# VectorE's order moved at the output projection, at the seam of two layers and at the router of a two-layer decoder trunk

## The chip, the core and the metric

One Trainium2 chip, one core. The time is the device time of one launch in microseconds (us). Engine names of the profile: PE is TensorE (PEld its weight loads), DVE VectorE, ACT ScalarE, POOL GpSimd, SP SyncE. A name with q (DVEq, ACTq) is the engine's instruction queue, where semaphore increments and waits run.

## The reference

512 tokens of width 1024 pass two residual layers, all in fp32:

```python
for layer in range(2):
    h = rms_norm(x, attn_norm[layer])
    x = x + (hgrn2_diff_mixer(h, ...) if layer % 2 == 0 else gla_mixer(h, ...))
    h = rms_norm(x, ffn_norm[layer])
    x = x + hierarchical_moe(h, ...)
```

Both mixers end with `merge_heads(rms_norm(o)) * silu(g)`, times an output weight of 1024x1024. The mixture of experts picks one of 4 groups and then 2 of its 4 experts for each token, with a weight from two softmaxes. Each of the 16 experts is `(silu(h @ w_gate) * (h @ w_up)) @ w_down` with 1024x512, 1024x512 and 512x1024 weights.

## The kernel before, in words

**Three products for one.** A large fp32 product is made of three faster fp32r products: each operand is split into a high part, which ScalarE rounds off by a copy to fp32r, and a low part, which VectorE makes as operand minus high part. `three` (lines 1091 to 1096) issues the products; one step of it covers 128 rows of the contraction. A wait for a "low half" is thus a wait for VectorE.

**Order by lists.** What each engine does in a layer up to the router is written as a list of steps (`mixer_steps`, `norm_steps`). Every engine walks the same list in order and does its own part of each step, so moving a step moves it on all of them, SP and GpSimd included. `with_splits` puts the four pieces ("split") of the next 1024x512 weight group ahead of the last two of the four product units (one unit is 128 rows of output) of a group. Queues are in order, and engines wait for each other by semaphores.

**Output projection.** For each of four token tiles i: step `out` makes the head outputs (TensorE) and, on ScalarE, VectorE and GpSimd, their norm: ScalarE squares into the single buffer `exp_tmp`, VectorE sums, GpSimd takes the power -0.5 (line 765), VectorE multiplies into G (line 1465). Step `oT` transposes G (TensorE, line 1120), copies the high half (ScalarE, line 902) and makes the low half (VectorE, line 1559). Its transposes use PSUM banks 2 and 3 in each tile, so tile i+1 needs the low half of tile i done. Step `wo` is the product (24 steps of TensorE) and the add to x (VectorE, line 1722). `gw` multiplies the gates by the norm weight (line 1604). `out` of tiles 0 and 2 and of 1 and 3 share PSUM banks. The first expert's gate weight is loaded by SP when `out` of tile 3 is done.

**Seam** (from layer 0's experts to layer 1's first product, `norm_steps(2)`). `x` i adds the two gathered expert rows of tile i to x (line 1510, two instructions), `p` i adds the last expert's rows (line 1519), which TensorE makes as a product with a one-hot matrix (line 1435, four instructions for a tile). `stat` i squares x (ScalarE), `h` i is the norm (lines 1454, 765, 1542), `hT` i its transpose and two halves. Before the change TensorE makes the products of all four `p` in a row ahead of the list, with banks 0-1, 4-5, 2-3 and again 4-5.

**Router and first expert.** VectorE, in order: one-hot matrices, `first_low(1, ...)` (low halves of the first expert's up weight, line 1529), `idx` to GpSimd, which gathers the first expert's rows by DMA; then token weights and the last expert's one-hot (lines 1783 to 1795, `last_ready`); then the *lists*: slots of each token and the list of further blocks (lines 1797 to 1829, `eid_ready`), 32 instructions; then `rows_T(0, 0)` and `rows_T(1, 1)`, the low halves of the gathered rows of experts 0 and 1 (line 1844); `low(GATE)`, four low halves of expert 1's gate weight (line 1836); `times_up(0)`, silu(gate) times up (line 1857, `act_ready`); then the expert loop, whose `block_ve` begins with `low(DOWN)`, four low halves of the down weight, and the low half of the activations (line 1869). TensorE, in order: rows 0 transposed, gate product of expert 0, rows 1 transposed, one-hot transposed (needs `last_ready`), up product 0; then in `block_pe(0)`: gate product of expert 1, in whose middle, after 12 of 24 steps, stand the transposes of expert 0's activations (`act_T`, needs `act_ready`), rows 2 transposed, down product 0, up product 1, and so on. `slot` and `eid` are read at the end of the experts only.

Of the kernel before, what the change touches and what calls it, by code (L numbers as in the profile page):

```python
# [87 lines left out]
def build(nc, t):  # L88
# [37 lines left out]
    def mixer_steps(l):  # L126
# [9 lines left out]
        if l == 0:  # L136
# [26 lines left out]
            steps += [dS[0], dS[1], out[0], fill.pop(0), dS[2], out[1], fill.pop(0)] + weighted[2:4]  # L163
        else:
# [19 lines left out]
        out, oT, wo = ([(*k, i) for i in range(NT)] for k in (("out", l), ("oT", l), ("wo", l, 0)))  # L184
        steps += [out[2], oT[0], out[3], oT[1], wo[0], oT[2], wo[1], oT[3], wo[2], wo[3]]
# [7 lines left out]
    def norm_steps(n):  # L193
# [4 lines left out]
        if n == 0:  # L198
# [3 lines left out]
        return [x[0], x[1], own[0], p[0], p[1], own[1], stat[0], h[0], own[2], own[3], x[2], hT[0], stat[1], halves[0],  # L202
                h[1], p[2], x[3], hT[1], stat[2], u[0], p[3], h[2], hT[2], stat[3], u[1], h[3], hT[3], u[2],
# [31 lines left out]
    with ctx:  # L235
# [207 lines left out]
        for l in range(NL):  # L443
# [59 lines left out]
            for i in range(NT):  # L503
                bk.plan(("P", l, i), ([0, 1], [4, 5], [2, 3], [4, 5])[i])
# [218 lines left out]
        def _(pool):  # L723
# [52 lines left out]
            for l in range(NL):  # L776
                for s in STEPS[l]:
# [6 lines left out]
                    elif s[0] == "out" or s[0] == "da" and s[2] >= 3 and (s[2] - 3) % NH == NH - 1:  # L784
# [28 lines left out]
        def _(sc):  # L813
# [41 lines left out]
            for l in range(NL):  # L855
# [7 lines left out]
                for s in STEPS[l]:  # L863
# [95 lines left out]
                    elif kind == "out":  # L959
                        head_norm(s, DVS[l])  # L960
# [126 lines left out]
        def _(pe):  # L1087
# [9 lines left out]

            for l in range(NL):
# [3 lines left out]
                for s in STEPS[l]:  # L1102
                    kind = s[0]
                    if kind in ("hT", "oT", "xT"):
# [10 lines left out]
                        for g in range(2):  # L1115
# [5 lines left out]
                            ins.then_inc(bk.filled(k), 1)  # L1121
                    elif kind == "alpha":
# [305 lines left out]
                pe.wait_ge(bk.freed(("lastT", l)), bk.uses[("lastT", l)][1])  # L1428
                for i in range(NT):
                    key = ("P", l, i)  # L1430
                    bk.acquire(pe, key)
                    for c in range(2):
                        if i == 0:
                            pe.wait_ge(y_ready, 2 * l + c + 1)
                        ins = pe.matmul(PS[:, bk.uses[key][0] + c], lastT[:, i * P:(i + 1) * P],
                                        y_last[0:CAP, c * GC:(c + 1) * GC], start=True, stop=True)
                    ins.then_inc(bk.filled(key), 1)
# [3 lines left out]
        def _(ve):  # L1441
# [81 lines left out]
            for l in range(NL):  # L1523
# [7 lines left out]
                for s in STEPS[l]:  # L1531
# [152 lines left out]
                    elif kind == "out":  # L1684
                        i = s[2]
                        dv = DVS[l]
                        head_norm(wide(s, dv), dv, lambda c: G[:, i, c * dv:(c + 1) * dv], G[:, i, 0:NH * dv])
# [95 lines left out]
                ve.wait_ge(r_eg, l + 1)  # L1783
                link(red(r["gsum"], r["eg"], AX, ALU.add))
                ve.wait_ge(r_e2, l + 1)
                link(ts(r["den"], r["e2"], 1.0, None, ALU.add))
                link(tt(r["den"], r["den"], r["gsum"], ALU.mult))
                link(ve.reciprocal(r["wt"][:, 0], r["den"]))
                link(tt(r["wt"][:, 1], r["wt"][:, 0], r["e2"], ALU.mult))
                link(tt(r["w_of"], r["OH"][:, :, :, NE - 1], r["wt"], ALU.mult))  # L1790
                link(tt(r["w_last"], r["w_of"][:, 0], r["w_of"][:, 1], ALU.add))
                for i in range(NT):
                    ins = ts(ohj[:, i], iota_f[:, 0:CAP], rank[:, i, NE - 1:NE], r["M"][:, i, NE - 1:NE], ALU.is_equal, ALU.mult)
                link(ins)
                ve.sem_inc(last_ready, 1)

                link(ts(r["nx"], total, float(CAP), None, ALU.is_gt))
                for m in range(2, FULLS + 1):
                    link(stt(r["nx"], total, float(m * CAP), r["nx"], ALU.is_gt, ALU.add))
                link(ve.tensor_tensor_scan(r["off"], ones[:, 0:NE], r["nx"], 0.0, ALU.mult, ALU.add))  # L1800
                link(tt(r["off"], r["off"], r["nx"], ALU.subtract))
                link(ts(r["q"], rank, float(CAP), None, ALU.is_ge))

                link(tt(r["ein"][:, 0], r["off"], iota_f[:, 0:NE], ALU.subtract))
                link(ts(r["ein"][:, 0], r["ein"][:, 0], float(NE - 1), None, ALU.add))
                link(tt(r["b"], r["q"], r["ein"][:, 0:1].broadcast_to([P, NT, NE]), ALU.mult))
                for m in range(2, FULLS + 1):
                    link(stt(r["q"], rank, float(m * CAP), r["q"], ALU.is_ge, ALU.add))
                link(tt(r["b"], r["b"], r["q"], ALU.add))
                link(tt(r["b"], r["b"], iota_f[:, 0:NE].unsqueeze(1).broadcast_to([P, NT, NE]), ALU.add))  # L1810
                link(stt(r["j"], r["q"], -float(CAP), rank, ALU.mult, ALU.add))
                for of, by in (("bc", "b"), ("jc", "j")):
                    link(tt(r["tA"], r["OH"], r[by].unsqueeze(1).broadcast_to(both), ALU.mult))
                    link(red(r[of], r["tA"], AX, ALU.add))
                link(stt(r["jz"], r["bc"], float(NE - 1), r["jc"], ALU.not_equal, ALU.mult))
                link(stt(r["sl"], r["bc"], float(CAP), r["jz"], ALU.mult, ALU.add))
                link(cp(slot[:], r["sl"]))

                it8 = iota_f[:, 0:16].unsqueeze(2).broadcast_to([P, 16, NE])
                off8 = r["off"].unsqueeze(1).broadcast_to([P, 16, NE])  # L1820
                nx8 = r["nx"].unsqueeze(1).broadcast_to([P, 16, NE])
                link(tt(r["ein"], it8, off8, ALU.subtract))
                link(tt(r["ein2"], r["ein"], nx8, ALU.is_lt))
                link(stt(r["ein2"], r["ein"], 0.0, r["ein2"], ALU.is_ge, ALU.mult))
                link(tt(r["ein2"], r["ein2"], iota_f[:, 0:NE].unsqueeze(1).broadcast_to([P, 16, NE]), ALU.mult))
                link(red(r["eidf"], r["ein2"], AX, ALU.add))
                link(red(r["eidf"][:, 15:16], r["nx"], AX, ALU.add))
                link(cp(eid[:], r["eidf"]))
                ve.sem_inc(eid_ready, 1)

# [54 lines left out]
                rows_T(0, 0)  # L1885
# [42 lines left out]
```

## Time and profile before

| | us |
|---|---|
| median of 3 runs | 1304.54 (1303.98 to 1304.84) |
| profiled execution, device time | 1303.31 |
| its span | 1301.5 |
| PE, PEld busy | 1171.5, 886.2 |
| DVE, ACT, POOL busy | 916.6, 682.2, 95.5 |

The profile is of one execution. Its span runs from the first to the last instruction; the device time holds 1.8 us more. The stages follow each other in time: mixer of layer 0 up to 288 us, its output projection and router product up to 346, lists and first expert up to 391, experts up to 670, seam up to 709, and then the same for layer 1 (output projection 902, lists 965, experts 1003 to 1284). A row of a timeline gives start, duration, engine, line, operation, output and inputs, shape, how many instructions are merged, and in brackets how long the engine had been idle before it and who ended that.

### The profile page before, as it was taken

To read this page: it belongs to the slowest core of one execution; us is meant where nothing else is said; L and a number is where in the kernel's file an instruction comes from. 1 tells how busy PE (TensorE), PEld (TensorE's weight loads), DVE (VectorE), ACT (ScalarE), POOL (GpSimd) and SP (SyncE) were. 2 spreads that over 40 slices of the span, in tenths; PEclk is the share of its full clock that TensorE was granted. 3 is DMA by queue.
4 is the path that set the end of the run, shared out by engine and by line. 5 is a ranking of instruction groups with operands and counts; after the bars stand their busy time and mean duration, and the time that the engine had idled before them with its cause. 6 is when DMAs were issued, how large, how long until landed. Compare 5 with 4: busy or idle time off the path is not lost.

```text
span 1301.5 us, 16716 instructions
## 1 busy us (share of the span) xinstructions
PE 1171.5 (90%) x5676; PEld 886.2 (68%) x5676; DVE 916.6 (70%) x1247; ACT 682.2 (52%) x853; POOL 95.5 (7%) x132
## 2 busy tenths in 40 slices
PE   5998889979759999999987999998966999999995
PEld 4776578868636767666646678887854766676663
DVE  4656658564568888888976247646566888888886
ACT  4336751133327878777743251122323877878771
POOL 1120000010010000000030000001000000000003
PEclk9999999989869999999997999999977999999998
DMA  6231110131479999999960131113167999999955
GB/s 218 90 87 65 65 65 1 65 129 66 162 271 344 392 392 394 386 396 395 338 214 1 69 98 52 65 66 130 65 231 256 354 393 395 393 388 392 391 203 206
DMA packets 129644, 282.51 MB, mean 217 GB/s; under 512 B 18976, under 2 KB 19488, under 8 KB 129584
## 3 DMA queue, kind: packets, MB, share of 16 engines
q1 hardware_dynamic: 119680, 246.98, 51.4%
q0 software_dynamic: 6112, 21.76, 5.1%
q10 hardware_dynamic: 3792, 12.98, 2.6%
q8 instruction: 36, 0.59, 0.2%
q14 instruction: 24, 0.20, 0.0%
HBM read 262.83 MB, written 18.87 MB: 216 GB/s over the span
## 4 chain that ended last, share of the span: by engine, by line
PE 60%; DVE 22%; issue 10%; ACT 5%; POOL 1%; DVEq 1%; DMA 0%; ACTq 0%
PE PS L1094 18%; PE PS L1096 17%; PE PS L1095 17%; DVE expert_w_low L1836 6%; PE PS L1183 3%; PE PS L1120 2%; DVE group_low L1575 1%; ACT weight_high L861 1%; DVE G L1465 1%; DVE xgT_low L1844 1%; POOL rstd L765 1%; PE PS L1293 1%; DVE sum_sq L1461 1%; DVE act L1857 1%; DVE x_sb L1519 1%
## 5 line engine op out<-in xcount | busy, mean ns | idle before, releaser
L1836 DVE TENSOR_TENSOR expert_w_low<-expert_w,weight_high 128x1024 fp32r<-128x1024 f32 x368 | 426.3, 1220 | 73.2 <-ACT weight_high L861 70.8
L861 ACT ACTIVATE weight_high<-expert_w 128x1024 fp32r<-128x1024 f32 x384 | 374.9, 1048 | 64.6 <-PE PS L1096 56.3
L1094 PE MATMUL PS<-weight_high,xgT_high 128*96 128x512 f32 x512 | 205.7, 402 | 12.7 <-DVEq L1846 9.3
L1096 PE MATMUL PS<-weight_high,xgT_low 128*96 128x512 f32 x512 | 202.8, 396 | 0.0
L1095 PE MATMUL PS<-expert_w_low,xgT_high 128*96 128x512 f32 x512 | 202.4, 395 | 0.0
L1094 PE MATMUL PS<-group_high,hT_high 128*128 128x512 f32 x416 | 173.1, 416 | 11.6 <-DVEq L1562 4.5
L1095 PE MATMUL PS<-group_low,hT_high 128*128 128x512 f32 x416 | 166.7, 401 | 0.0
L1096 PE MATMUL PS<-group_high,hT_low 128*128 128x512 f32 x416 | 166.7, 401 | 0.0
L1094 PEld LDWEIGHTS PS<-weight_high,xgT_high 128*96 128x96 f32 x512 | 83.3, 163 | 47.4 <-DVEq L1846 9.9
L1094 PE MATMUL PS<-weight_high,actT_high 128*96 128x512 f32 x256 | 103.8, 405 | 9.1 <-DVEq L1871 8.5
L1575 DVE TENSOR_TENSOR group_low<-group_w,group_high 128x1024 fp32r<-128x1024 f32 x68 | 80.7, 1222 | 43.9 <-ACT group_high L885 41.2
L1096 PEld LDWEIGHTS PS<-weight_high,xgT_low 128*96 128x96 f32 x512 | 83.3, 163 | 36.6
L1095 PEld LDWEIGHTS PS<-expert_w_low,xgT_high 128*96 128x96 f32 x512 | 83.7, 164 | 33.6
L1096 PE MATMUL PS<-weight_high,actT_low 128*96 128x512 f32 x256 | 101.3, 396 | 0.0
L1095 PE MATMUL PS<-expert_w_low,actT_high 128*96 128x512 f32 x256 | 101.0, 394 | 0.0
L1094 PEld LDWEIGHTS PS<-group_high,hT_high 128*128 128x128 f32 x416 | 80.5, 193 | 29.5 <-issue 5.2
L1096 PEld LDWEIGHTS PS<-group_high,hT_low 128*128 128x128 f32 x416 | 79.9, 192 | 18.9
L1095 PEld LDWEIGHTS PS<-group_low,hT_high 128*128 128x128 f32 x416 | 80.5, 193 | 16.3
L885 ACT ACTIVATE group_high<-group_w 128x1024 fp32r<-128x1024 f32 x68 | 69.1, 1054 | 27.9 <-PE PS L1096 23.8
L1183 PEld LDWEIGHTS PS<-Q,K 128*128 128x128 f32 x512 | 61.0, 192 | 11.4 <-DVE K L1653 4.3
L1183 PE MATMUL PS<-Q,K 128*128 128x64 f32 (+1 forms) x512 | 61.4, 273 | 6.4 <-DVEq L1629 2.9
L1094 PEld LDWEIGHTS PS<-weight_high,actT_high 128*96 128x96 f32 x256 | 41.5, 162 | 30.4 <-DVEq L1871 5.9
(244 smaller groups left out, 1457.9 us busy)
## 6 DMA issues: line engine op xcount, KB each, us to landing
expert_w<-in_moe_w_gate SPq DMA_DIRECT2D x32, 2048.0 KB, 11.5
expert_w<-in_moe_w_up SPq DMA_DIRECT2D x32, 2048.0 KB, 10.4
expert_w<-in_moe_w_down SPq DMA_DIRECT2D x32, 2048.0 KB, 10.9
group_w<-in_even_w_in SPq DMA_DIRECT2D x6, 2048.0 KB, 7.8
group_w<-in_odd_w_in SPq DMA_DIRECT2D x6, 2048.0 KB, 7.9
y_rows<-yb ACTq DMA_DIRECT2D x30, 384.0 KB, 5.7
group_w<-in_even_w_out SPq DMA_DIRECT2D x2, 2048.0 KB, 7.7
h_rows<-h SPq DMA_DIRECT2D x8, 512.0 KB, 10.8
```

The source lines that it names most:

```text
L765: pool.tensor_tensor(dst, dst, neghalf[:, 0:dst.shape[-1]], ALU.pow).then_inc(root_ready, 1)
L861: act_(hi, w, ACT.Copy).then_inc(w_hi, 1)
L885: act_(hi, w, ACT.Copy).then_inc(g_hi_ready, 1)
L1094: pe.matmul(out, ah, bh, start=first, stop=False)
L1095: pe.matmul(out, ah, bl, start=False, stop=False)
L1096: return pe.matmul(out, al, bh, start=False, stop=final)
L1120: ins = pe.transpose(bank(k)[:, c * P:(c + 1) * P], src[:, i, d:d + P], ident[:])
L1183: ins = pe.matmul(out, K[:, c, cols], q, start=True, stop=True)
L1293: ins = pe.matmul(bank(key)[:, i * NR:(i + 1) * NR], xT[:, k, i * P:(i + 1) * P], rw[:, k, :], start=k == 0, stop=k == KD - 1)
L1461: link(red(ss[:, 0:NH], e, AX, ALU.add))
L1575: tt(lo, w, hi.bitcast(F32), ALU.subtract).then_inc(g_lo_ready, 1)
L1836: tt(lo, w, hi.bitcast(F32), ALU.subtract).then_inc(w_lo, 1)
```

## The change

Four edits of order; no arithmetic changes.

1. The norm becomes a step `norm` of its own, apart from the product `out`. At the output projection the list is now `oT` 0, `out` 2, `oT` 1, `norm` 2, `out` 3, `norm` 3, `wo` 0. Ahead of it, `norm` 0 and `norm` 1 stand behind the next product unit of the last group (in layer 1 `norm` 1 behind `gw` too).
2. At the seam: `p` 0 ahead of the first split; `hT` 0, `stat` 1, the first half product and `h` 1 ahead of `x` 2; `hT` 1 and `h` 2 ahead of `x` 3.
3. TensorE's products of `p` move from the end of the experts into the list, each at its step (function `rows_of_last`); their banks are now 2-3, 4-5, 2-3, 4-5.
4. At the router VectorE does `rows_T(0, 0)` ahead of the token weights, and the lists after `low(GATE)`.

```diff
@@ mixer_steps, even layer
-            steps += [dS[0], dS[1], out[0], fill.pop(0), dS[2], out[1], fill.pop(0)] + weighted[2:4]
+            norm = [("norm", l, i) for i in range(NT)]
+            steps += [dS[0], dS[1], out[0], fill.pop(0), norm[0], dS[2], out[1], fill.pop(0), norm[1]] + weighted[2:4]
@@ odd layer
-                    steps += [halves[unit][0], ("dS", l, 2), ("out", l, 0), unit] + weighted(n - 1) + [("out", l, 1)]
-            steps += weighted(len(rest) - 1)
+                    steps += ([halves[unit][0], ("dS", l, 2), ("out", l, 0), unit] + weighted(n - 1)
+                              + [("norm", l, 0), ("out", l, 1)] + weighted(n) + [("norm", l, 1)])
@@ both layers
-        steps += [out[2], oT[0], out[3], oT[1], wo[0], oT[2], wo[1], oT[3], wo[2], wo[3]]
+        steps += [oT[0], out[2], oT[1], norm[2], out[3], norm[3], wo[0], oT[2], wo[1], oT[3], wo[2], wo[3]]
@@ norm_steps
-        return [x[0], x[1], own[0], p[0], p[1], own[1], stat[0], h[0], own[2], own[3], x[2], hT[0], stat[1], halves[0],
-                h[1], p[2], x[3], hT[1], stat[2], u[0], p[3], h[2], hT[2], stat[3], u[1], h[3], hT[3], u[2],
+        return [x[0], x[1], p[0], own[0], p[1], own[1], stat[0], h[0], own[2], own[3], hT[0], stat[1], halves[0], h[1],
+                x[2], p[2], hT[1], stat[2], u[0], h[2], x[3], p[3], hT[2], stat[3], u[1], h[3], hT[3], u[2],
                 halves[3], u[3]]
@@ banks of the last expert's rows
-                bk.plan(("P", l, i), ([0, 1], [4, 5], [2, 3], [4, 5])[i])
+                bk.plan(("P", l, i), ([2, 3], [4, 5])[i % 2])
@@ GpSimd, ScalarE, VectorE: the norm's part goes from step "out" to step "norm"
-                    elif s[0] == "out" or s[0] == "da" and ...
+                    elif s[0] == "norm" or s[0] == "da" and ...
@@ TensorE
+            def rows_of_last(l, i):
+                key = ("P", l, i)
+                if i == 0:
+                    pe.wait_ge(bk.freed(("lastT", l)), bk.uses[("lastT", l)][1])
+                bk.acquire(pe, key)
+                for c in range(2):
+                    if i == 0:
+                        pe.wait_ge(y_ready, 2 * l + c + 1)
+                    ins = pe.matmul(PS[:, bk.uses[key][0] + c], lastT[:, i * P:(i + 1) * P],
+                                    y_last[0:CAP, c * GC:(c + 1) * GC], start=True, stop=True)
+                ins.then_inc(bk.filled(key), 1)
...
+                    elif kind == "p":
+                        rows_of_last(l - 1, s[2])
...
-                pe.wait_ge(bk.freed(("lastT", l)), bk.uses[("lastT", l)][1])
-                for i in range(NT):
-                    key = ("P", l, i)
...
+            for kind, i in added:
+                if kind == "p":
+                    rows_of_last(NL - 1, i)
@@ VectorE, router
                 first_low(1, range(2, SPLITS))
-                (token weights, last one-hot, last_ready)
-                (lists: nx, off, q, b, j, bc, jc, slot, ein, eid, eid_ready)
...
                 rows_T(0, 0)
+                (token weights, last one-hot, last_ready)
                 rows_T(1, 1)
                 low(GATE)
+                (lists: nx, off, q, b, j, bc, jc, slot, ein, eid, eid_ready)
                 times_up(0)
                 expert_loop(ve, block_ve, link)
```

## Rows read from the trace of the kernel before

**Rows 1.** The page: the chain that ended last, share of the span by engine.
```profile
PE 60%; DVE 22%; issue 10%; ACT 5%; POOL 1%; DVEq 1%; DMA 0%; ACTq 0%
```

**Rows 2.** Windows by stage: length, busy time of each engine, granted clock, DMA share, GB/s.
```profile
391.00:660.00 269.00, 265.46 (x1247) 187.65 (x1248) 233.43 (x223) 212.36 (x239) 14.41 (x26) 1.00 1.01 377
```

**Rows 3.** Timeline, layer 0, from the lists to the first gate product.
```profile
364.87 0.17 DVE L1797 TENSOR_SCALAR r_nx<-r_R 128x16 f32<-128x16 f32 x1
...
369.66 0.81 ACT L1002 ACTIVATE xgT_high<-PS 128x768 fp32r<-128x768 f32 x1 [15.17 <-PE PS L1328]
...
373.48 0.17 DVE L1828 CAST eid<-r_eidf 128x16 int32<-128x16 f32 x1
373.80 0.96 DVE L1844 TENSOR_TENSOR xgT_low<-PS,xgT_high 128x768 fp32r<-128x768 f32 x1
374.86 0.23 PEld L1094 LDWEIGHTS PS<-weight_high,xgT_high 128*96 128x96 f32 x1 [5.54 <-DVEq L1846]
```

**Rows 4.** The same place in layer 1.
```profile
983.07 0.81 ACT L1002 ACTIVATE xgT_high<-PS 128x768 fp32r<-128x768 f32 x1 [16.34 <-PE PS L1328]
...
986.03 0.96 DVE L1844 TENSOR_TENSOR xgT_low<-PS,xgT_high 128x768 fp32r<-128x768 f32 x1
```

**Rows 5.** Timeline, layer 0, from low(GATE) to the first down product.
```profile
391.22 0.69 DVE L1857 TENSOR_TENSOR act<-PS,ex 96x512 f32<-96x512 f32 x1 [0.16 <-ACTq L1010]
...
391.36 0.44 PE L1094 MATMUL PS<-weight_high,xgT_high 128*96 128x512 f32 x1 [1.82 <-issue]
...
392.49 4.63 DVE L1836 TENSOR_TENSOR expert_w_low<-expert_w,weight_high 128x1024 fp32r<-128x1024 f32 x4 [0.58 <-ACT weight_high L861]
...
394.18 0.50 PE L1337 MATMUL PS<-ident,act 96*128 96x96 f32 x4
...
397.04 0.55 DVE L1869 TENSOR_TENSOR actT_low<-PS,actT_high 128x384 fp32r<-128x384 f32 x1
...
397.87 0.46 PE L1094 MATMUL PS<-weight_high,actT_high 128*96 128x512 f32 x1
```

**Rows 6.** TensorE at its lower clock and back: gate product 0; after a 2.64 us wait.
```profile
376.68 0.63 PE L1095 MATMUL PS<-expert_w_low,xgT_high 128*96 128x512 f32 x1
377.11 0.63 PE L1096 MATMUL PS<-weight_high,xgT_low 128*96 128x512 f32 x1
...
380.16 0.39 PE L1095 MATMUL PS<-expert_w_low,xgT_high 128*96 128x512 f32 x1
380.39 0.40 PE L1096 MATMUL PS<-weight_high,xgT_low 128*96 128x512 f32 x1
...
894.54 0.70 PE L1217 MATMUL PS<-h,AT 128*128 128x256 f32 x2 [2.64 <-DVEq L1688]
```

**Rows 7.** Timeline, output projection of layer 0.
```profile
278.94 2.36 DVE L1575 TENSOR_TENSOR group_low<-group_w,group_high 128x1024 fp32r<-128x1024 f32 x2 [0.25 <-DVE G L1465]
...
286.16 1.53 DVE L1559 TENSOR_TENSOR hT_low<-PS,hT_high 128x512 fp32r<-128x512 f32 x2 [0.24 <-DVE G L1465]
287.06 1.94 PE L1120 MATMUL PS<-ident,G 128*128 128x128 f32 x8 [6.10 <-DVEq L1561]
...
288.65 0.78 PE L1094 MATMUL PS<-group_high,hT_high 128*128 128x512 f32 x1
```

**Rows 8.** Timeline, first output product of layer 1.
```profile
901.92 0.48 PE L1094 MATMUL PS<-group_high,hT_high 128*128 128x512 f32 x1
```

**Rows 9.** Timeline, seam.
```profile
674.21 1.23 DVE L1575 TENSOR_TENSOR group_low<-group_w,group_high 128x1024 fp32r<-128x1024 f32 x1 [1.83 <-ACT group_high L885]
...
678.43 2.20 PE L1435 MATMUL PS<-y_last,last_onehot_T 96*128 96x512 f32 x4 [1.64 <-DVEq L1521]
...
683.92 2.67 DVE L1510 SCALAR_TENSOR_TENSOR x_sb<-yg,r_wt,x_sb 128x1024 f32<-128x1024 f32 x2
...
688.24 0.80 PE L1094 MATMUL PS<-group_high,hT_high 128*128 128x512 f32 x1 [4.48 <-DVEq L1562]
...
708.59 0.38 PE L1120 MATMUL PS<-ident,h 128*128 128x128 f32 x2
```

More of the change, by code:

```diff
@@ L783, in _ @@
                         power(dstd[:, s[3] % 2])
-                    elif s[0] == "out" or s[0] == "da" and s[2] >= 3 and (s[2] - 3) % NH == NH - 1:
+                    elif s[0] == "norm" or s[0] == "da" and s[2] >= 3 and (s[2] - 3) % NH == NH - 1:
                         power(rstd[:, 0:NH])
@@ L958, in _ @@
                             sc.sem_inc(bk.freed(key), 1)
-                    elif kind == "out":
-                        head_norm(s, DVS[l])
+                    elif kind == "norm":
+                        head_norm(("out", *s[1:]), DVS[l])
                     elif kind == "wo" and s[2] == 1:
@@ L1683, in _ @@
                         ve.sem_inc(bk.freed(s), 1)
-                    elif kind == "out":
+                    elif kind == "norm":
                         i = s[2]
                         dv = DVS[l]
+                        s = ("out", *s[1:])
                         head_norm(wide(s, dv), dv, lambda c: G[:, i, c * dv:(c + 1) * dv], G[:, i, 0:NH * dv])
@@ L1791, in _ @@
[L1791 to L1814, printed above, removed]
@@ L1885, in _ @@
                 rows_T(0, 0)
+                ve.wait_ge(r_eg, l + 1)
+                link(red(r["gsum"], r["eg"], AX, ALU.add))
+                ve.wait_ge(r_e2, l + 1)
+                link(ts(r["den"], r["e2"], 1.0, None, ALU.add))
+                link(tt(r["den"], r["den"], r["gsum"], ALU.mult))
+                link(ve.reciprocal(r["wt"][:, 0], r["den"]))
+                link(tt(r["wt"][:, 1], r["wt"][:, 0], r["e2"], ALU.mult))
+                link(tt(r["w_of"], r["OH"][:, :, :, NE - 1], r["wt"], ALU.mult))
@@ L1886, in _ @@
+                link(tt(r["w_last"], r["w_of"][:, 0], r["w_of"][:, 1], ALU.add))
+                for i in range(NT):
+                    ins = ts(ohj[:, i], iota_f[:, 0:CAP], rank[:, i, NE - 1:NE], r["M"][:, i, NE - 1:NE], ALU.is_equal, ALU.mult)
+                link(ins)
+                ve.sem_inc(last_ready, 1)
                 rows_T(1, 1)
                 low(GATE)
+                link(ts(r["nx"], total, float(CAP), None, ALU.is_gt))
+                for m in range(2, FULLS + 1):
+                    link(stt(r["nx"], total, float(m * CAP), r["nx"], ALU.is_gt, ALU.add))
@@ new lines, in _ @@
+                for m in range(2, FULLS + 1):
+                    link(stt(r["q"], rank, float(m * CAP), r["q"], ALU.is_ge, ALU.add))
+                link(tt(r["b"], r["b"], r["q"], ALU.add))
+                link(tt(r["b"], r["b"], iota_f[:, 0:NE].unsqueeze(1).broadcast_to([P, NT, NE]), ALU.add))
+                link(stt(r["j"], r["q"], -float(CAP), rank, ALU.mult, ALU.add))
+                for of, by in (("bc", "b"), ("jc", "j")):
+                    link(tt(r["tA"], r["OH"], r[by].unsqueeze(1).broadcast_to(both), ALU.mult))
+                    link(red(r[of], r["tA"], AX, ALU.add))
@@ new lines, in _ @@
+                link(stt(r["jz"], r["bc"], float(NE - 1), r["jc"], ALU.not_equal, ALU.mult))
+                link(stt(r["sl"], r["bc"], float(CAP), r["jz"], ALU.mult, ALU.add))
+                link(cp(slot[:], r["sl"]))
+                it8 = iota_f[:, 0:16].unsqueeze(2).broadcast_to([P, 16, NE])
+                off8 = r["off"].unsqueeze(1).broadcast_to([P, 16, NE])
+                nx8 = r["nx"].unsqueeze(1).broadcast_to([P, 16, NE])
+                link(tt(r["ein"], it8, off8, ALU.subtract))
```

44 lines of the change are left out of this document (14 added, 30 removed).

## The prediction, made before the changed kernel was run

> **What bounds the kernel now.** I read the chain of waits first: TensorE holds 60% of it and VectorE 22% [rows 1]. The reader is to see in it that VectorE sets the end in places only. The windows by stage say where: in the expert stage TensorE is busy 265.46 of 269 us at full clock [rows 2], so an idle stretch of TensorE there, or just ahead of it, is lost time, and little of it can be won back. TensorE waits for VectorE at the output projection, the seam and the router, the places this change touches; there I went through the timeline of TensorE, VectorE and ScalarE instruction by instruction. The method for each place is the same: write VectorE's new order, give every instruction its old duration, and find when the next product of TensorE may start.
>
> **Router, the gain.** ScalarE has the high half of the first gathered rows at 369.66 + 0.81 = 370.47, but VectorE is in the lists and makes the low half at 373.80 [rows 3]. Moved ahead, it starts at once: 373.80 - 370.50 = 3.3 us earlier in layer 0. In layer 1 it is 986.03 - 983.92 = 2.1 us [rows 4]. The first gate product moves by as much. The token weights now run beside that product and cost nothing: it needs them only for the one-hot's transposes behind it. If that product were as short as the slack, the last one-hot would be late; it is 24 steps, over 5 us.
>
> **Router, the loss.** The lists take 373.65 - 364.87 = 8.8 us of VectorE [rows 3], 32 short instructions. Before, they stood where VectorE would have waited for the gather anyway, for all but the 3.3 (2.1) us above. Now they stand between the low halves of expert 1's gate weight and `times_up(0)`. I take the old times and shift at the end. Before: `times_up` at 391.22, gate product 1 from 391.36, transposes of the activations at 394.18, down product at 397.87 [rows 5]. The activations had a slack of 394.18 - (391.22 + 0.69) = 2.3 us. With the lists in front, `times_up` runs from 391.3 + 8.8 = 400.1 to 400.8: the transposes start at 400.9 and TensorE stands idle for 6.7 us. Queued behind `times_up` on VectorE are the four low halves of the down weight (4.63 us) and the low half of the activations (0.55 us) [rows 5]. With 0.2 us after `times_up` they run from 401.0 to 406.1, and the down product starts at 406.2 instead of 397.87: 8.3 us late. ScalarE cannot cover this, its high halves were only 0.58 us from being VectorE's limit [rows 5].
>
> The idle stretch also halves TensorE's clock. At the lower of its two levels (1.2 GHz) steps stand 377.11 - 376.68 = 0.43 us apart, at 2.4 GHz 380.39 - 380.16 = 0.23 us [rows 6]; after the wait of 4 to 5 us ahead of gate product 0 the clock was back only at 379.65, some 11 steps later. The 12 steps behind the transposes, about 10 of them slow, end near 406.1, and the next transposes (8 at 0.1 us) near 406.8, 0.5 us after VectorE's path. So 8.8 us is my value for each layer. Ends: 8.3 us if the clock stays or returns in time; 9.9 us if all 12 steps and the 8 transposes run at the lower level. Net: layer 0 8.8 - 3.3 = +5.5, layer 1 8.8 - 2.1 = +6.7, together +12.2 us. Lower end: 2 x 8.3 - 5.4 = 11.2, and if the earlier start also spares the 11 slow steps of gate product 0 (11 x 0.2 = 2.2 us a layer), 6.8. Upper end: 2 x 9.9 - 5.4 = 14.4.
>
> Here a rule of the Trainium skill speaks against my 0.5 us: "TensorE: Matmul & The Clock Gate", section "Loop structure matters more than you think", has a VectorE copy out of PSUM between two tiles as something that does not cool TensorE. In this trace a wait of 2.64 us for VectorE's queue ends in steps at the lower clock [rows 6], so the trace does not agree where TensorE waits for the copy. By the rule the sum would be about 1 us less; I go by the row.
>
> **Output projection.** Layer 0: before, VectorE did the norms of tiles 1 and 2 ahead of the low half of tile 0 (286.16), the transposes of tile 1 waited 6.10 us for its bank (287.06), and the first `wo` product started at 288.65 [rows 7]. Now the norm of tile 2 comes later, but two things take back much of it: the norm of tile 1 stands behind two splits (2.36 us [rows 7]) that it preceded, and `out` 3, 16 matmuls that ran in the gap before, stands between the transposes and `wo`. Worked through: norm 1 ends at 280.8, low half 0 runs 282.6 to 284.1, transposes 283.4 to 285.1, `out` 3 at the lower clock 3.5 us to 288.6 less what warms up: `wo` at 287.5, 1.1 us earlier. Bounds: `out` 3 at full clock -2.2, a wait more at tile 1 +1. Layer 1: norm 0 now waits for ScalarE's last gate, TensorE idles about 3 us ahead of the transposes of tile 0, and low half 0 ends near 897.5; transposes and `out` 3 (3.5 us) follow, `wo` near 901.8 against 901.92 [rows 8]: 0, bounds -1.3 and +1.5. SP's load of the first expert's weight is issued some 8 us later than before and still has over 10 us in hand before ScalarE reads it. Sum -1.1 us, between -3.5 and +2.5.
>
> **Seam.** `p` 0 goes into the 1.83 us in which VectorE waited for ScalarE's first high half [rows 9]: -1.2 us for `h` 0. `x` 2 (2.67 us) leaves the path of `hT` 0 [rows 9]. The first product then starts at 688.24 - 1.2 - 2.6 = 684.5, 3.8 us earlier. But `p` 2 now waits for TensorE's product of it, four instructions of 0.43 us [rows 9] behind the half product, which runs at the lower clock: from 684.5 to 689.6, product to 691.3, and then on VectorE `p` 2, low half 1, norm 2, `x` 3, `p` 3, low half 2, norm 3. The transposes of tile 3, 708.59 before [rows 9], come at 703.6 if TensorE warms up early and at 705.4 if not: between -5.0 and -3.2; I take -4.0, and as bounds -5.8 (no wait for the product at all) and -2.0. GpSimd's powers and ScalarE's squares only follow. At the end of the kernel the products of `p` 2 and 3 now wait for a bank, but two `x` instructions of 1.3 us stand ahead of each add: 0.
>
> **Sum.** -1.1 - 4.0 + 12.2 = +7.1 us on the profiled execution's 1303.3 us (1301.5 span and 1.8 around it): 1310.4. The median of the runs shown is 1.2 us above that execution, so 1311.6.
>
> **Rivals.**
> 1. *The router costs less than I say and cancels with the rest.* The earlier start spares the slow steps of gate product 0, and the stall falls on 8.3: +6.8, seam -5.0, output -1.1: +0.7, 1305.2. For it: the two slow stretches differ by more than 1 us between the layers, so the clock's return is partly chance. Against it: the gather of rows 1 must land first, which leaves room for 1 us at most.
> 2. *Faster: the expert stage takes the stall back.* If the stage's pace is set by the weights' transfers and not by TensorE, work that starts late catches up, the 17.6 us of loss vanish and the gains stay: -1.1 - 4.0 - 5.4 = -10.5, 1294.0. For it: the DMA engines are busy all the time at 377 GB/s [rows 2]. Against: with TensorE busy 98.7% of the stage there is only 3.5 us of idle time to give, so at most 3.5 us a layer comes back; with that, +0.1. It decides from the point where ScalarE's high halves wait for DMA instead of TensorE, and none does in the rows.
> 3. *Worse: the front edits fail too.* The transposes of tile 1 or `p` 2 hold TensorE as long as before and cool it: seam -2.0, output +2.5, router +14.4: +14.9, 1319.4.
>
> **How the numbers follow.** The forecast 0.60, rival 1 0.17, rival 2 0.11 (part of it only as far as no change), rival 3 0.12. A measurement tells 0.2% from no change, 2.6 us: below 1301.9 faster, above 1307.2 slower. The forecast's own range is 1307.5 to 1315.5 and nearly all slower. Slower 0.70, same 0.19, faster 0.11. The range 1303.5 to 1317 holds forecast, rival 1 and half of rival 3.
>
> **What would show it.** In the changed profile the low half of rows 0 follows ScalarE's high half at once, in both layers; TensorE has a gap of 6 to 7 us in the middle of gate product 1, ended by VectorE's queue, with slow steps behind it, and VectorE none between `low(GATE)` and the lists; the expert stage has its old length from the first down product on. The transposes of tile 3 of the seam come 3 to 5 us earlier against the end of the experts. I am wrong if that gap is under 3 us, if the expert stage after it is shorter than before, or if the seam gives nothing.

## The result, and the profile after

The changed kernel took 1315.01 us (median of 4 runs, 1312.23 to 1315.9) against 1304.26 us (4 runs) for the kernel before in the same session: a ratio of 1.0076, 95% interval 1.0063 to 1.0089: slower, by less than 1%. By the medians the change costs 10.8 us, where the forecast had 7.1. Its profiled execution took 1315.9 us, with a span of 1314.0 against 1301.5.

The page's chain after, answering to [rows 1]; each entry is an engine's share of the span:

```profile
PE 60%; DVE 20%; issue 10%; ACT 5%; DMA 2%; POOL 1%; DVEq 1%; ACTq 0%; POOLq 0%
```

It hardly differs from before: 1% of the span cannot be found in shares. So I cut both spans at instructions that exist in both, GpSimd's copies of the index columns (copy k follows the transposes of gathered rows k, one per expert), its powers for the norms, and its first gathers of expert outputs. Lengths in us, one profiled execution each (the experiments' kernels stand with them; what they change is told below):

```
from ... to                              before   after  router   no     lists   lists   best
                                                          only  router  in gap  behind
start .. first norm behind wo, layer 0   326.43  327.41  326.49  324.71  327.29  327.80  324.69
.. rows 0 transposed                      43.38   44.10   43.61   44.21   43.83   44.20   43.90
.. rows 1 transposed (gate product 0)     13.90   10.93   10.36   14.06   11.05   10.85   11.07
.. rows 2 transposed (gate product 1)     14.55   22.71   23.94   14.60   14.55   14.60   14.56
.. first gather of outputs (experts)     262.30  262.11  262.18  262.14  262.43  272.33  262.11
.. first norm behind wo, layer 1         278.10  277.53  281.43  276.45  276.31  276.45  275.09
.. rows 0 transposed, layer 1             44.55   43.45   43.82   44.59   44.52   44.42   44.36
.. rows 1 transposed                      12.15    9.88   10.11   13.69   10.47   10.46   11.24
.. rows 2 transposed                      14.26   23.55   23.69   14.26   14.26   14.26   14.27
.. first gather of outputs (experts)     262.43  262.38  262.34  262.40  263.15  272.58  263.10
.. end                                    29.45   29.95   28.23   29.99   29.84   28.35   28.41
```

Between before and after, two stages are longer by far: gate product 1 in layer 0 (+8.2) and in layer 1 (+9.3). The product ahead of each is shorter (-3.0, -2.3). The 262 us of the expert stage that follow have kept their length, to 0.2 us.

The gain, in the timeline after (start, duration, engine, line, operation, idle time before it and what ended it), answering to [rows 3]:

```profile
371.37 0.81 ACT L1003 ACTIVATE xgT_high<-PS 128x768 fp32r<-128x768 f32 x1 [15.36 <-PE PS L1344]
...
372.21 0.96 DVE L1806 TENSOR_TENSOR xgT_low<-PS,xgT_high 128x768 fp32r<-128x768 f32 x1 [8.36 <-ACT xgT_high L1003]
...
373.28 0.74 PE L1095 MATMUL PS<-weight_high,xgT_high 128*96 128x512 f32 x1 [1.95 <-DVEq L1808]
```

The low half starts 0.03 us behind ScalarE's high half, and VectorE had been idle for 8.36 us before it: the time in which the lists used to run. The loss, answering to [rows 5]:

```profile
385.16 4.63 DVE L1798 TENSOR_TENSOR expert_w_low<-expert_w,weight_high 128x1024 fp32r<-128x1024 f32 x4 [1.05 <-ACT weight_high L862]
...
392.68 0.40 PE L1097 MATMUL PS<-weight_high,xgT_low 128*96 128x512 f32 x1
...
398.29 0.17 DVE L1895 CAST eid<-r_eidf 128x16 int32<-128x16 f32 x1
398.69 0.69 DVE L1819 TENSOR_TENSOR act<-PS,ex 96x512 f32<-96x512 f32 x1 [0.22 <-DVE eid L1895]
399.54 0.87 PE L1353 MATMUL PS<-ident,act 96*128 96x96 f32 x4 [6.46 <-issue]
399.62 4.63 DVE L1798 TENSOR_TENSOR expert_w_low<-expert_w,weight_high 128x1024 fp32r<-128x1024 f32 x4 [0.24 <-DVE act L1819]
400.11 0.72 PE L1095 MATMUL PS<-weight_high,xgT_high 128*96 128x512 f32 x1
400.63 0.63 PE L1096 MATMUL PS<-expert_w_low,xgT_high 128*96 128x512 f32 x1
...
402.76 0.39 PE L1095 MATMUL PS<-weight_high,xgT_high 128*96 128x512 f32 x1
403.00 0.39 PE L1096 MATMUL PS<-expert_w_low,xgT_high 128*96 128x512 f32 x1
...
404.17 0.55 DVE L1831 TENSOR_TENSOR actT_low<-PS,actT_high 128x384 fp32r<-128x384 f32 x1
...
404.82 0.47 PE L1095 MATMUL PS<-weight_high,actT_high 128*96 128x512 f32 x1
```

VectorE runs without a pause: low halves, lists to 398.46, `times_up`, four low halves, low half of the activations. TensorE stands idle for 6.46 us in the middle of gate product 1. The row names "issue" as what ended it, since the profile found no semaphore for it; VectorE's `act` row ends 0.16 us earlier and is what it waited for. The down product starts at 404.82 where it was 397.87. In layer 0 six steps behind the transposes stand 0.43 us apart and the rest 0.23; in layer 1, after a wait of the same length, all twelve do, and its stage loses 1.1 us more:

```profile
1014.96 0.87 PE L1353 MATMUL PS<-ident,act 96*128 96x96 f32 x4 [6.50 <-issue]
...
1020.32 0.51 PE L1097 MATMUL PS<-weight_high,xgT_low 128*96 128x512 f32 x1
```

The expert stage as a window (length, then busy us of TensorE, its weight loads, VectorE, ScalarE, GpSimd, then granted clock, DMA share, GB/s), shifted by 7 us to stand against [rows 2]:

```profile
398.00:667.00 269.00, 264.33 (x1235) 186.88 (x1236) 233.85 (x225) 208.60 (x234) 14.41 (x26) 0.99 0.99 369
```

The seam, answering to [rows 9]: ScalarE's copies of the last expert's output, the product of tiles 0 and 1, then the half product, the product of tile 2 with VectorE's wait for it, and the transposes of tile 3.

```profile
679.03 1.30 ACT L1038 ACTIVATE y_last<-PS 96x512 f32<-96x512 f32 x2 [8.24 <-PE PS L1097]
680.55 3.67 PE L1108 MATMUL PS<-y_last,last_onehot_T 96*128 96x512 f32 x8 [1.55 <-ACTq L1040]
...
694.31 0.79 PE L1095 MATMUL PS<-group_high,hT_high 128*128 128x512 f32 x1 [2.28 <-DVEq L1571]
...
699.17 0.63 PE L1097 MATMUL PS<-group_high,hT_low 128*128 128x512 f32 x1
699.60 1.94 PE L1108 MATMUL PS<-y_last,last_onehot_T 96*128 96x512 f32 x4
...
701.57 1.28 DVE L1528 SCALAR_TENSOR_TENSOR x_sb<-PS,r_w_last,x_sb 128x1024 f32<-128x1024 f32 x1 [2.52 <-PE PS L1108]
...
715.13 1.09 PE L1134 MATMUL PS<-ident,h 128*128 128x128 f32 x8 [1.43 <-DVE h L1551]
```

Before, the first product ran at 671.41 and waited 0.82 us for ScalarE; now it waits 1.55 us:

```profile
671.41 5.39 PE L1435 MATMUL PS<-y_last,last_onehot_T 96*128 96x512 f32 x12 [0.82 <-ACTq L1038]
```

It took banks 0 and 1 before, free after the first copy of the last output, and takes 2 and 3 now, free after the second. From the first product to the transposes of tile 3 it was 708.59 - 671.41 = 37.2 us and is 715.13 - 680.55 = 34.6. Of these 2.6 us, 3.1 are gained up to the half product (688.24 - 671.41 = 16.8, now 694.31 - 680.55 = 13.8), and 0.5 is given back behind it.

The output projection of layer 0, answering to [rows 7]:

```profile
285.29 1.53 DVE L1568 TENSOR_TENSOR hT_low<-PS,hT_high 128x512 fp32r<-128x512 f32 x2
286.18 1.94 PE L1134 MATMUL PS<-ident,G 128*128 128x128 f32 x8 [4.93 <-DVEq L1570]
...
290.67 0.48 PE L1095 MATMUL PS<-group_high,hT_high 128*128 128x512 f32 x1
```

`wo` starts at 290.67 against 288.65, though nothing of the change lies ahead: the first 102 us of this execution, whose code is the same, are 2.65 us longer (up to GpSimd's eighth power for the differential heads, 105.12 against 102.47). Against that `wo` starts 0.6 us earlier, and the first norm behind it comes 1.7 us earlier: `out` 3 has taken the slow steps that stood at the head of `wo` before (first step 0.48 us instead of 0.78), which is the other 1.0 us. In layer 1 `wo` starts at 907.95 against 901.92, with 6.54 us of delay brought along from the seam: 0.5 us earlier.

### The profile page after: what moved, and what is told of

The parts are those of the page before. It is cut to its first block, busy times and chain, and to the rows that moved or that the text cites. A ratio compares the mean times of both kernels' runs of the same rounds, so it can differ in the third digit from the quotient of the medians.

```text
span 1314.0 us, 16731 instructions
## 1 busy us (share of the span) xinstructions
PE 1179.4 (90%) x5676; PEld 891.1 (68%) x5676; DVE 916.5 (70%) x1247; ACT 683.1 (52%) x853; POOL 94.6 (7%) x132
## 4 chain that ended last, share of the span: by engine, by line
PE 60%; DVE 20%; issue 10%; ACT 5%; DMA 2%; POOL 1%; DVEq 1%; ACTq 0%; POOLq 0%
PE PS L1095 17%; PE PS L1097 16%; PE PS L1096 16%; DVE expert_w_low L1798 7%; PE PS L1199 3%; PE PS L1134 1%; DVE group_low L1584 1%; ACT weight_high L862 1%; PE PS L1309 1%; DMA xg<-h_rows,idx 1%; DVE xgT_low L1806 1%; DVE G L1474 1%; PE PS L1108 1%; DVE x_sb L1528 1%; DVE hT_low L1568 1%
```

## The experiments

The median of the kernel before was 1304.95 us beside the first four, 1304.83 beside the next four and 1305.13 beside the last two, against 1304.26 beside the change itself. A difference between the change and one of these kernels thus carries up to 0.9 us of that.

**router_only**: the kernel before with the router's part of the change alone.

```diff
+ rows_T(0, 0)
  (token weights)
+ rows_T(1, 1)
+ low(GATE)
  (lists)
- rows_T(0, 0)
- rows_T(1, 1)
- low(GATE)
  times_up(0)
```

> The kernel before with the router edit alone: rows_T(0, 0) ahead of the token weights, the lists between low(GATE) and times_up(0). Theory A (the lists hold up times_up, each layer pays 8 us and gets back 2 to 3): +12 us against before, range 10 to 14, and in both layers a gap of TensorE over 6 us in the middle of gate product 1. Theory B (the router is about even, and the loss of the whole change comes from the seam, the banks of the last expert's rows and the end): within 3 us of before.

Measured 1318.99 us (4 runs), ratio 1.0111 [1.0096, 1.0126]: +14.0. In the table its router stages are -3.5 and +9.4 in layer 0, -2.0 and +9.4 in layer 1, +13.2 together. The router's part alone makes more than the whole loss.

**no_router**: the changed kernel with the router's order as before (the same diff backwards).

> The changed kernel with VectorE's order at the router as before; output projection, seam and banks as changed. Theory A: the rest of the change is worth -2 to 0 us against before (output projection -2, seam -2, end of the kernel +1 to +2.5 because the first product of the last expert's rows waits for a later bank). My prediction's own terms say -5. Theory B: +8 us or more against before.

Measured 1302.84 us (12 runs), ratio 0.9985 [0.9976, 0.9993]. The other two parts gain 2.1 us; the router costs 1315.0 - 1302.8 = 12.2 us by the medians, 11.9 by the two ratios.

**lists_in_gap**: the changed kernel with the lists where VectorE is idle beside gate product 0.

```diff
  rows_T(0, 0)
  (token weights)
- rows_T(1, 1)
- low(GATE)
  (lists)
+ rows_T(1, 1)
+ low(GATE)
  times_up(0)
```

> The changed kernel with the lists moved from behind low(GATE) to directly behind the token weights, so between rows_T(0, 0) and rows_T(1, 1), where VectorE stood idle for 7.3 us. Theory A: the gain of the early low half stays (3.3 and 2.1 us) and the stall goes: 17 us under the changed kernel, 5 to 8 us under before; the lists end some 1.5 us after the gate product 0 and hide behind the up product. Theory B: no more than 3 us under the changed kernel.

Measured 1299.36 us (6 runs), ratio 0.9949 [0.9937, 0.9962]: 15.6 us less than the change, where 17 had been expected. In the timeline the lists overrun the gap: ScalarE has the second rows' high half at 382.04 + 0.81 = 382.85, VectorE makes the low half 2.1 us later:

```profile
371.81 0.96 DVE L1806 TENSOR_TENSOR xgT_low<-PS,xgT_high 128x768 fp32r<-128x768 f32 x1 [8.04 <-ACT xgT_high L1003]
...
382.04 0.81 ACT L1003 ACTIVATE xgT_high<-PS 128x768 fp32r<-128x768 f32 x1 [10.26 <-PE PS L1344]
...
384.30 0.18 DVE L1893 CAST eid<-r_eidf 128x16 int32<-128x16 f32 x1
384.97 0.96 DVE L1806 TENSOR_TENSOR xgT_low<-PS,xgT_high 128x768 fp32r<-128x768 f32 x1 [0.50 <-DVE eid L1893]
...
390.72 0.68 DVE L1819 TENSOR_TENSOR act<-PS,ex 96x512 f32<-96x512 f32 x1
```

The gain of the earlier first product is kept (11.05 us in the table) and the stall is gone (14.55): the overrun costs TensorE nothing, since this low half is needed for gate product 1 only. The gap is not a new one. In the kernel before VectorE stood idle there for 9.67 us; the change, with the token weights moved into it, left 7.28:

```profile
384.42 0.96 DVE L1844 TENSOR_TENSOR xgT_low<-PS,xgT_high 128x768 fp32r<-128x768 f32 x1 [9.67 <-ACT xgT_high L1002]
```

**lists_behind_act**: the changed kernel with `times_up(0)` ahead of the lists. It parts "the activations come late" from "everything behind the lists on VectorE comes late".

```diff
  low(GATE)
+ times_up(0)
  (lists)
- times_up(0)
  expert_loop(ve, block_ve, link)
```

> The changed kernel with the lists moved one step on, behind times_up(0), so ahead of the low halves of the down weight. If the price is set by all of VectorE's path to the down product, as my prediction has it (8.3 us of 8.8, and 0.5 for the clock): the gap in the middle of gate product 1 is gone, TensorE waits instead ahead of the down product by 8 us, and the time is that of the changed kernel, -1 to +1 us. Rival: the price is that of act being late only (6.7 us a layer): then -10 us or more against the changed kernel.

Measured 1316.94 us (6 runs), ratio 1.0088 [1.0073, 1.0102]: no better than the change, 1.9 us above it by the medians where at most 1 had been expected. TensorE's timeline: the transposes of the activations are on time, and the idle stretch has moved to the down product.

```profile
393.35 0.49 PE L1353 MATMUL PS<-ident,act 96*128 96x96 f32 x4
396.45 0.82 PE L1344 MATMUL PS<-ident,xg 96*128 96x96 f32 x8
405.44 0.74 PE L1095 MATMUL PS<-weight_high,actT_high 128*96 128x512 f32 x1 [8.16 <-DVEq L1833]
```

So the price is that of VectorE's whole path, here 8.16 us idle and 10.0 us with the slow steps behind it (272.33 - 262.30 in the table). Moving the one instruction that TensorE waits for ahead of the lists helps nothing while the next five stay behind them.

**bank01**: the changed kernel with the banks of the last expert's products as before.

```diff
- bk.plan(("P", l, i), ([2, 3], [4, 5])[i % 2])
+ bk.plan(("P", l, i), ([0, 1], [4, 5], [2, 3], [4, 5])[i])
```

> The changed kernel with the product of p 0 on banks 0 and 1 again (1: 4-5, 2: 2-3, 3: 4-5, as before). If the banks matter: its first instruction follows the first of ScalarE's two copies of the last expert's output, 0.7 us earlier than in the changed kernel, at the seam and at the end: -1.4 us, and up to -2.5 if p 1 at the end follows. If they do not: 0 us. This is close to what the measurement can tell; the waits of the trace decide.

Measured 1312.4 us (6 runs), ratio 1.0063 [1.0046, 1.0081], whose interval overlaps that of the change; 2.6 us less by the medians. The trace shows what the banks do, again 0.82 us of wait for the first copy:

```profile
676.60 1.30 ACT L1038 ACTIVATE y_last<-PS 96x512 f32<-96x512 f32 x2 [8.24 <-PE PS L1097]
...
677.39 3.67 PE L1108 MATMUL PS<-y_last,last_onehot_T 96*128 96x512 f32 x8 [0.82 <-ACTq L1039]
```

That the wait is the banks' is shown: from ScalarE's copy to the first product it is 1.51 to 1.53 us in all six traces with the new banks and 0.78 to 0.79 in all six with the old, at the seam and at the end. What it costs is not. The end stage is 28.46 us here instead of 29.95, but seam_only and lists_behind_act, with the new banks, have 28.25 and 28.35. From the first product to the end it is 18.4 us in the change, no_router and after_p and 16.7 in seam_only, lists_in_gap and lists_behind_act, whose code there is the same. The difference is TensorE's clock behind the same wait, here over 4 us of the products in the change and then in seam_only:

```profile
1296.00:1300.00 4.00, 4.00 (x7) 1.67 (x6) 2.41 (x2) 0.00 (x0) 0.00 (x0) 0.63 0.91 322
1285.00:1289.00 4.00, 3.42 (x8) 1.44 (x8) 1.80 (x2) 0.37 (x1) 1.32 (x1) 1.00 0.92 350
```

With the old banks it is 17.1 to 17.6 us from the first product to the end, so at the higher clock the later start is made up there. Whether the longer wait makes the lower clock likelier (three of six traces against none of six) is open.

**op_only** and **seam_only**: the kernel before with the output projection's part alone, and with the seam's part alone (its list of steps, the products in that list, the banks). The cores of their diffs:

```diff
- steps += [out[2], oT[0], out[3], oT[1], wo[0], ...]
+ steps += [oT[0], out[2], oT[1], norm[2], out[3], norm[3], wo[0], ...]
```

```diff
- return [x[0], x[1], own[0], p[0], ... own[3], x[2], hT[0], stat[1], halves[0], h[1], p[2], x[3], hT[1], ...
+ return [x[0], x[1], p[0], own[0], ... own[3], hT[0], stat[1], halves[0], h[1], x[2], p[2], hT[1], ...
```

> The kernel before with the output projection's edit alone (norms behind the next product units, oT and out in the new order); seam, banks and router as before. From the changed kernel's trace: the first wo product 1.7 us earlier in layer 0 and 0.5 us earlier in layer 1, nothing given back: -2 us against before. My prediction said -1.1. Rival: out 3 now stands behind the transposes of tile 1 and takes the gain back: 0.

> The kernel before with the seam's edit alone: new order of x, p, h and hT, the products of p in TensorE's list, banks 2-3 and 4-5. My prediction said -4.0 for the seam and 0 for the end. From the changed kernel's trace the seam itself gives -1.9 (the first product of the last expert's rows starts 0.7 us later for its bank, the half product stays at the lower clock and p 2 waits for its product behind it), and the end loses 1 to 2 us: 0 in sum, -2 to +1.

Measured: op_only 1305.55 us (12 runs, 1297.87 to 1308.33), ratio 0.9999 [0.9985, 1.0014], where 2 us less had been expected; seam_only 1303.16 us (12 runs), ratio 0.9987 [0.9978, 0.9995], 1.7 us less, inside its expectation. The expectation of op_only calls the 1.7 us the start of `wo`; they are those of the first norm behind it. The stretch from the middle of the mixer (the power named above) to this norm, 223.96 us before, is 222.42 in op_only, 222.29 in the change and 222.68 in seam_only, which has no edit there: 1.3 of the 1.7 us can be had by chance. Its second part is steadier: from the start of `wo` to the norm it is 36.7 to 36.8 us in all nine traces with the edit and 37.8 to 38.7 in the three without. The rival of op_only's expectation, that `out` 3 takes the gain back, is not what the trace shows; its number is right, but the interval of the time, 2 us to each side, can neither show nor exclude a gain of this size.

**best**: the changed kernel with the lists split, the part up to `r_j` ahead of `rows_T(0, 0)` in the idle time before the gather lands, the rest beside gate product 0, and the banks as in bank01.

```diff
+ (token weights; lists up to r_j)
  rows_T(0, 0)
- (token weights)
- rows_T(1, 1)
- low(GATE)
- (lists)
+ (lists from the sums over experts on)
+ rows_T(1, 1)
+ low(GATE)
  times_up(0)
```

> The changed kernel with the lists cut in two, both in idle time of VectorE: token weights and the lists up to the block numbers while the gather of rows 0 is under way, the slots and the list of blocks between rows_T(0, 0) and rows_T(1, 1); and p 0 on banks 0 and 1. Against the kernel with all the lists in the second gap: 0 to -2 us (the bank 0.7 us at the seam and at the end, and the second gap no longer overrun). Against before: -6 to -8 us. Rival: the bank and the overrun cost nothing, then the same as lists_in_gap, -5.6.

Measured 1294.53 us (6 runs), ratio 0.9925 [0.9912, 0.9938]: 0.8% faster than before and 4.8 us below lists_in_gap, where I had expected 2 at most. VectorE now has slack on both sides:

```profile
367.63 0.22 DVE L1875 SCALAR_TENSOR_TENSOR r_j<-r_q,r_R 128x64 f32<-128x64 f32 x1
369.36 0.96 DVE L1806 TENSOR_TENSOR xgT_low<-PS,xgT_high 128x768 fp32r<-128x768 f32 x1 [1.51 <-ACT xgT_high L1003]
...
374.96 0.17 DVE L1893 CAST eid<-r_eidf 128x16 int32<-128x16 f32 x1
380.37 0.96 DVE L1806 TENSOR_TENSOR xgT_low<-PS,xgT_high 128x768 fp32r<-128x768 f32 x1 [5.24 <-ACT xgT_high L1003]
```

But the table gives the split nothing: the router's stages are as long as in lists_in_gap (11.07 and 14.56 against 11.05 and 14.55). The 4.8 us lie elsewhere in these two traces: 2.6 in the first stage, where the code is the same, 1.2 from the first gather of outputs to the first norm of layer 1, and 1.4 at the end. The 2.6 are the first 102 us again (105.03 against 102.46), with TensorE's clock at 0.94 between 78 and 106 us in lists_in_gap and 1.00 in best. Of the 1.4 at the end, the copies of the last output alone come 1.6 us later against the first gather in lists_in_gap, under the same code. The banks explain 0.7 us at the seam. So the split is not shown to gain anything over lists_in_gap, and most of the difference between the two traces stands in stretches with the same code; how much of that is in the medians of six runs each is open.

**after_p** and **best_p**: the change, and best, with TensorE issuing the products of tiles 1 to 3 together again, ahead of the transposes of tile 0. They test my reading of the seam, that VectorE's 2.52 us of wait ahead of `p` 2 are what is missing there.

```diff
  elif kind == "p":
-     rows_of_last(l - 1, s[2])
+     for i in ([0], [1, 2, 3], [], [])[s[2]]:
+         rows_of_last(l - 1, i)
```

> The changed kernel with the same edit of TensorE's order and nothing else (the banks of the products as in the change). Theory: the wait of 2.52 us ahead of p 2 is gone, 1312.5 (1311 to 1313.5), and the seam alone is worth about -4 us as predicted at first. Rival: another wait takes its place, 1315.0.

> The kernel of run best with one more edit: TensorE issues the products of tiles 1, 2 and 3 of the last expert together, as before the change, ahead of the transposes of tile 0; VectorE keeps the new order. Theory (the seam's missing gain is VectorE waiting for the product of tile 2, which stands behind the half product at the lower clock): VectorE's wait of 2.85 us ahead of p 2 is gone, the half product comes up to 1 us sooner, the transposes of tile 3 come about 2.5 us earlier against h 0, and the kernel takes 1292.0 (1291 to 1293) where best took 1294.5. Rival (the seam is paced by the round of norm, powers, transposes and high halves, and p 2 only fills an idle stretch of it): p 2 runs earlier but low half 1 waits instead for ScalarE's high half, the transposes of tile 3 move under 0.7 us, 1294.5.

Measured: after_p 1315.61 us (5 runs), ratio 1.0080 [1.0066, 1.0093]; best_p 1294.72 us (5 runs), ratio 0.9921 [0.9908, 0.9935]. Both medians are where they were without the edit, though the wait did go. Neither pair alone excludes 2.2 us, since each ratio is uncertain by 1.7 us to each side; both together make so much unlikely. VectorE and TensorE in best_p:

```profile
674.79 1.98 PE L1108 MATMUL PS<-y_last,last_onehot_T 96*128 96x512 f32 x4 [0.76 <-DVEq L1531]
...
684.08 2.67 DVE L1520 SCALAR_TENSOR_TENSOR x_sb<-yg,r_wt,x_sb 128x1024 f32<-128x1024 f32 x2
686.86 1.28 DVE L1529 SCALAR_TENSOR_TENSOR x_sb<-PS,r_w_last,x_sb 128x1024 f32<-128x1024 f32 x1
688.95 1.53 DVE L1569 TENSOR_TENSOR hT_low<-PS,hT_high 128x512 fp32r<-128x512 f32 x2 [0.81 <-ACT hT_high L903]
...
700.98 1.09 PE L1134 MATMUL PS<-ident,h 128*128 128x128 f32 x8 [1.41 <-DVE h L1552]
```

From the first product to the transposes of tile 3 it is now 700.98 - 668.64 = 32.3 us where best has 34.5, and 32.4 in after_p where the change has 34.6: 2.2 us less, twice. So the rival of both expectations falls in its mechanism (the transposes of tile 3 move by 2.2 us and not by under 0.7) and is right in its number. In best_p the stretch from the last norm of the seam to the first norm behind `wo` is 1.0 us longer (232.53 against 231.52), and TensorE's granted clock over the 64 us behind the seam is 0.97 where best has 1.00. But 1.00 and 0.95 also stand there in before and router_only, and 1.00 and 0.97 in the change and no_router, whose code is the same in that stretch. The trace of best_p has besides 2.0 us more in the first 102 us and 1.1 more at the end than that of best, both under the same code. Whether the clock takes this gain back or covers it by chance, these runs cannot tell.

## Why the prediction was right, and where its terms were off

The forecast was 1311.6 us; the time was 1315.01, inside the range of 1303.5 to 1317.0, and at the upper edge of the forecast's own range (1307.5 to 1315.5). The mechanism, lists that hold up VectorE's whole queue ahead of the down product, is shown by router_only, no_router, lists_in_gap and lists_behind_act. That its size comes out to 0.1 us is partly luck, and the seam was mis-sized. Point by point, with stage lengths of the profiled executions:

- **Router, gain**: forecast 3.3 and 2.1 us. The stages of gate product 0 are 3.0 and 2.3 us shorter. Right, but in layer 1 only to 1 or 2 us: with the router's order as before that stage took 12.15 us in before and 12.83, 13.69 and 13.92 in seam_only, no_router and op_only, by the number of steps at the lower clock (8 in before, 11 in the last two).
- **Router, loss**: forecast 8.8 us for each layer, as VectorE's whole queue shifted by the lists (8.3) and a clock step (0.5). Measured 8.2 and 9.3, sum 17.5 against 17.6: the clock step was nothing in layer 0 and twice its size in layer 1, and the two errors cancel. Net +12.2 forecast, +12.2 in the table (5.2 and 7.0) against before, +10.5 in the table against no_router, and about 12 by the medians of the change and no_router. lists_behind_act shows that it is the whole queue that counts and not the one late activation. TensorE idled 6.46 and 6.50 us (forecast 6.7); the transposes and 6 steps behind them in layer 0, 12 in layer 1, ran at the lower of its levels (0.43 us apart), where the forecast had about 10.
- **The rule on the clock**, which spoke against the 0.5 us (the Trainium skill, "TensorE: Matmul & The Clock Gate", section "Loop structure matters more than you think": a VectorE copy between tiles does not cool TensorE; in the page's loop the next matmuls follow at once). Where TensorE has to wait for VectorE, as here, the trace does not agree: the steps stand 0.43 us apart after 6.46 us, and at the seam after 5.85 and 2.28 us with only transposes between. What the slow steps cost differs: nothing in layer 0, where VectorE's path ended later (8.2 us in all), and about 1 us in layer 1, where the down product starts 1.1 us behind the low half.
- **Output projection**: forecast -1.1 and 0 for the start of `wo`, traces -0.6 and -0.5, and -1.7 for the norm behind it in layer 0, since `wo` then runs at the higher clock from its first step, which the forecast had left out. In the time of op_only nothing. Inside its bounds, and too small to be measured here.
- **Seam**: forecast -4.0, measured 34.6 - 37.2 + 0.7 for the later first product = -1.9, just outside the lower bound of -2.0. This is the term that was mis-sized, by 2.1 us in three parts of about 0.7. First, the new banks, which I had read in the diff and never set against ScalarE's second copy. Second, the way from there to the half product, 13.8 us where the forecast has 684.5 - 671.41 = 13.1: `h` 0 came 0.9 us sooner and not 1.2, and the half product started 0.6 us behind the low half where before it was 0.2. Third, the way from the half product to the transposes of tile 3, 20.8 us: that is the forecast's own late case (705.4 - 684.5 = 20.9), of which it took the middle. The wait of `p` 2 for its product was in the forecast; `p` 2 started 7.3 us behind the half product against 6.8. Without that wait (after_p) the seam stands at 32.4 - 37.2 + 0.7 = -4.1. That this is the forecast's figure is chance: the forecast had the wait in, and gave -5.8 as the bound without it.
- **End**: forecast 0, measured +0.5 (29.95 against 29.45). My argument, that two instructions of 1.3 us stand ahead of each add, passed over the first product, which comes 0.7 us later. But the stage itself is 29.45, 28.23 and 27.98 us in before, router_only and op_only, whose end is the same, and 28.25 to 29.99 with the new banks; these traces do not show a cost of the change here.
- **Rest**: the first 102 us, with unchanged code, were 2.65 us longer in this execution. The forecast 1310.4 for this execution plus 2.1 for the seam, 0.5 for the end and 2.65 makes 1315.7, against 1315.9; the smaller differences cancel. The 2.65 and the 0.5 are not shown to be costs of the change, so of the 3.7 us by which the medians' difference (10.8) exceeds the forecast (7.1) only the seam's 2.1 have a cause.

Rival 1 (the router costs less) falls with the 17.5 us. Rival 2 (the expert stage takes the stall back) falls most clearly: 262.3 us before, 262.1 after, with 269 us of window holding 264 us of TensorE. Rival 3 was right about one thing, that `p` 2 still holds VectorE, and wrong about the output projection.

## What to carry to other kernels

On an engine that works its queue in order, short work that nobody needs yet costs nothing in a stretch where the engine waits, and its full length once it stands in a stretch where the engine paces another; before moving 32 short instructions, look at what is queued behind their new place down to the next product, not only at the instruction that is waited for. Before moving such work, look for the idle time that is there: here VectorE had 9.67 us of idle time beside gate product 0 even before the change, and the lists of 8.8 us could go there, with 2.1 us of overrun that nothing waited for. A saving of a few tenths of a per cent read from one trace is not yet one in the time: here 2.2 us were plainly gone from a stretch, twice, and the medians, good to 1.7 us to each side, did not move.

## What had not been expected of the hardware

- A stretch with the same instructions differs from execution to execution: the first 102 us took 102.3 to 102.6 us in before, router_only, op_only, no_router, bank01 and best, and 104.5 to 105.4 in after, seam_only, lists_in_gap, lists_behind_act, after_p and best_p, with nothing in between. TensorE's granted clock between 78 and 106 us is 1.00 in each of the first six and 0.94 in each of the others; in the change its steps at 17.7 us and at 92.5 us stand 0.43 us apart.
- The time at the lower clock does not follow from the length of the wait ahead of it: after 6.46 us idle in layer 0, 6 steps stood 0.43 us apart, after 6.50 us in layer 1, 12; at the seam, after waits of 5.85 and 2.28 us with only transposes between, all 12 steps of the half product did.
- The granted clock over the 64 us behind the seam was 1.00, 0.97 or 0.95, up to 3 us of time, also between kernels with the same code there. At the end of the kernel the same products behind the same wait of 1.56 us ran at 0.63 in the change and at 1.00 in seam_only over 4 us, 1.7 us of time.
